# An encoder layer on one core: two of every three feed-forward tiles 4 to 15 by seven block products, with half of their weight sums made by accumulating transfers

## What is computed

```python
def swiglu(h, w_gate, w_up, w_down):          # D_MODEL 1024, D_FF 2816
    return (jax.nn.silu(h @ w_gate) * (h @ w_up)) @ w_down
h = layer_norm(DN_ALPHA * h + 0.5 * swiglu(h, ffn1_w_gate, ffn1_w_up, ffn1_w_down), g1, b1)
h = layer_norm(DN_ALPHA * h + token_mixer(h, ...), gm, bm)
h = layer_norm(DN_ALPHA * h + 0.5 * swiglu(h, ffn2_w_gate, ffn2_w_up, ffn2_w_down), g2, b2)
```

## Time and profile before

| | |
|---|---|
| median of 3 runs | 1043.09 us (1040.11 to 1043.65) |
| the profiled execution, its own time | 1039.09 us |
| its span, first to last instruction | 1037.3 us |
| granted TensorE clock, mean | 0.988 |
| busy PE / DVE / ACT / POOL | 970.1 / 760.3 / 494.8 / 52.1 us |
| bytes moved by transfers | 89.26 MB, mean 86 GB/s |

### The profile page before, as it was taken

One profiled execution on the slowest core, in us unless ns is written; L12 is line 12 of the kernel. 1 busy time (PEld: TensorE's weight loads), 2 busy tenths in 40 slices (PEclk: granted clock), 3 DMA queues, 4 the chain that ended last, 5 costly groups with the idle time before them and its releaser, 6 DMA issues.

```text
span 1037.3 us, 17455 instructions
## 1 busy us (share of the span) xinstructions
PE 970.1 (94%) x7131; PEld 693.6 (67%) x7131; DVE 760.3 (73%) x1344; ACT 494.8 (48%) x707; POOL 52.1 (5%) x96
## 2 busy tenths in 40 slices
PE   2999999999999999999997899899899999999995
PEld 1888888888788886875565437665566644434584
DVE  6877766577987676877567978878777667889634
ACT  5576655244422245763335752567666434342214
POOL 0000000000020000000000010001000000011000
PEclk9999999999999999999998989999999999999999
DMA  5233322233334300212111012122332322424002
GB/s 210 84 111 122 114 91 94 77 109 120 112 119 152 123 2 1 82 42 71 52 41 42 1 35 88 49 74 82 123 122 88 117 82 82 163 99 170 15 1 82
DMA packets 24993, 89.26 MB, mean 86 GB/s; under 512 B 3035, under 2 KB 5427, under 8 KB 24915
## 3 DMA queue, kind: packets, MB, share of 16 engines
q1 hardware_dynamic: 23904, 87.17, 24.6%
q10 hardware_dynamic: 1011, 0.99, 0.3%
HBM read 86.05 MB, written 2.10 MB: 85 GB/s over the span
## 4 chain that ended last, share of the span: by engine, by line
PE 57%; DVE 25%; ACT 10%; issue 5%; DMA 2%; POOL 1%; SPq 0%; ACTq 0%; DVEq 0%
PE PS L732 9%; PE PS L682 9%; PE PS L758 8%; PE PS L853 7%; PE PS L652 6%; DVE cmax L1793 5%; PE PS L760 4%; DVE wsp L1815 4%; PE PS L763 3%; ACT wsp L1295 2%; PE PS L827 1%; DVE big L2020 1%; ACT H L1289 1%; PE PS L1133 1%; PE PS L976 1%
## 5 line engine op out<-in xcount | busy, mean ns | idle before, releaser
L652 PE MATMUL PS<-xs,wsp 128*128 128x264 f16 (+1 forms) x1344 | 195.4, 307 | 5.6 <-DVE wsp L1815 4.5
L652 PEld LDWEIGHTS PS<-xs,wsp 128*128 128x128 f16 x1344 | 131.0, 98 | 68.9 <-DVE wsp L1815 7.9
L732 PE MATMUL PS<-xs,wsp 128*128 128x264 f16 (+1 forms) x864 | 130.9, 310 | 0.0
L1793 DVE TENSOR_REDUCE cmax<-stage 128x1 f32<-128x2048 f32 (+2 forms) x47 | 120.2, 2557 | 4.5 <-DMA stage<-in_w_out 3.6
L1295 ACT ACTIVATE wsp<-stage,wscale 128x2048 f16<-128x2048 f32 (+2 forms) x34 | 70.8, 2081 | 100.0 <-DVE wscale L1779 78.1
L732 PEld LDWEIGHTS PS<-xs,wsp 128*128 128x128 f16 x864 | 84.5, 98 | 39.9
L2681 POOL PARTITION_ALL_REDUCE call<-cmax x73 | 48.8, 669 | 894.8 <-DVE cmax L1793 652.4
L1815 DVE SCALAR_TENSOR_TENSOR wsp<-stage,wscale,wsp 128x2048 f16<-128x2048 f32 (+2 forms) x34 | 83.3, 2449 | 12.8 <-ACT wsp L1295 12.8
L758 PE MATMUL PS<-big,arena 128*128 128x264 f16 (+1 forms) x792 | 89.4, 274 | 0.0
L758 PEld LDWEIGHTS PS<-big,arena 128*128 128x128 f16 x792 | 77.5, 98 | 11.5
L763 PE MATMUL PS<-big,wsp 128*128 128x264 f16 x660 | 75.1, 276 | 1.4 <-DVE big L2020 1.3
(11 more groups left out here) (267 smaller groups left out, 1421.8 us busy)
## 6 DMA issues: line engine op xcount, KB each, us to landing
stage<-in_gate SPq DMA_DIRECT2D x44, 512.0 KB, 3.7
stage<-in_up SPq DMA_DIRECT2D x44, 512.0 KB, 4.5
stage<-in_down SPq DMA_DIRECT2D x32, 704.0 KB, 5.3
stage<-in_w_in SPq DMA_DIRECT2D x16, 512.0 KB, 4.6
stage<-in_w_out SPq DMA_DIRECT2D x8, 512.0 KB, 4.2
X<-in_x SPq DMA_DIRECT2D x4, 512.0 KB, 6.2
out_T<-H SPq DMA_DIRECT2D x16, 128.0 KB, 1.7
stage<-in_w_in SPq DMA_DIRECT2D x2, 576.0 KB, 4.8
```

The source lines that it names most:

```text
L652: return nc.tensor.matmul(dst, w, x, start=k == 0 and wp + xp == 0, stop=k == KD - 1 and xp == 1)
L732: mm = nc.tensor.matmul(dst, w, x, start=k == 0 and wp + xp == 0, stop=k == KD - 1 and xp == 1)
L1793: nc.vector.tensor_reduce(cmax[:, one], stage[:, slot, 0:cols], AX.X, ALU.max, apply_absolute_value=True).then_inc(w_max, 1)
```

## The change

Tiles 4 to 15 (`MIXED`) are worked in groups of three: tiles 4, 5, 7, 8, 10, 11, 13 and 14 by seven products, tiles 6, 9, 12 and 15 plain. That is 8 seven-product tiles in a feed-forward in place of 6. The tiles no longer go in pairs: each tile's products run one behind the other.

* **Buffers.** The chunks of tiles 4 to 15 rotate over three buffers: the two of `stage` and a third in the arena (`raw_third`). Tile 4's chunk is loaded into the third, ahead of tile 3's chunk in SP's program; in the first feed-forward behind a wait on `tok_sq`, in the second behind a wait for `x_ready` to reach its last count, which is when the last low part of the normed tokens is written.
* **Sums.** Two of the four weight sums come from transfers that POOL issues with `accum_op=ALU.add`: B11 is added onto the up block in the raw buffer (giving T1), and B22 onto a second copy of the up block, that SP loads for this (256 KB more for each seven-product tile), giving T3. Each moves 128 x 512 float32, 256 KB, inside SBUF. T2 and T4 stay on DVE as two instructions of 512 columns. Some of the sums have the other sign than before; the token sums and one scale (`up_scale`, `xinv_neg`) are negated for it.
* **Splits.** A seven-product tile has one high and one low part instruction of 2048 columns (`raw_split_hi`, `raw_split_lo`) and one of each of 1536 columns (`sums_split_hi`, `sums_split_lo`). PE's product 0 waits for the first pair alone (`raw_ready`).
* **Bounds.** `weight_sum` on ACT serves tiles 3 to 17; `chunk_max` on DVE falls away for tiles 16 and 17.

```diff
+MIXED = range(4, 16)
-SEVEN_AT = [4, 6, 8, 10, 12, 14]
+SEVEN_AT = [4, 5, 7, 8, 10, 11, 13, 14]
-SUMMED_FROM = 3
+SUMMED = range(3, 18)
+N_BUF = 3
...
+            def load_mixed(f, m):
+                i = m - MIXED[0]
+                if i == 0:
+                    if f == 0:
+                        sp.wait_ge(tok_sq, N_TOK)
+                    else:
+                        sp.wait_ge(x_ready, ln_tile(2, 2 * KD))
+                elif i < N_BUF:
+                    sp.wait_ge(w_ready, GU[f] + i + 2)
+                else:
+                    free_home(f, m - N_BUF)
+                done = mixed_loaded[buf(m)]
+                sp.dma_start(home(f, m)[:, 0:KD * P], gate[f][m]).then_inc(done, 16)
+                sp.dma_start(home(f, m)[:, KD * P:GU_COLS], up[f][m]).then_inc(done, 16)
+                if m not in SEVEN_AT:
+                    return
+                if N_BUF <= i < 2 * N_BUF:
+                    sp.wait_ge(s_ready2, 4 * f + 4)
+                elif i >= 2 * N_BUF:
+                    sp.wait_ge(w_ready, GU[f] + m - N_BUF + 1)
+                sp.dma_start(sums_at(m)[:, 0:4 * P], up[f][m][:, 0:4 * P]).then_inc(done, 16)
...
+                for m in range(2, 4):
+                    if m == 3:
+                        load_mixed(f, MIXED[0])
+                    sp.wait_ge(w_ready, GU[f] + m - 1)
+                    load_gu(f, m, (GU[f] + m) % 2)
+                for m in MIXED[1:]:
+                    load_mixed(f, m)
...
                 for m in MIXED:        # ACT, ffn(f)
+                    if m + 1 in SEVEN_AT:
+                        raw_split_hi(f, m + 1)
+                    else:
+                        gu_split_hi(f, m + 1)
+                    if m in SEVEN_AT:
+                        p1_copy(f, m)
+                    if m - 1 in SEVEN_AT:
+                        seven_gate(f, m - 1, 1)
+                    elif m > MIXED[0]:
+                        silu_tile(GU[f] + m - 1, (GU[f] + m - 1) % 2, m - 1, (m - 1) % 2, f)
+                    if m + 1 in SEVEN_AT:
+                        sums_split_hi(f, m + 1)
+                    if m + 3 in SUMMED:
+                        weight_sum(f, m + 3)
+                    hidden_sum(f, m - 1)
+                    if m in SEVEN_AT:
+                        seven_gate(f, m, 0)
...
+                for m in MIXED:        # DVE, ffn(f)
+                    if m - 1 in SEVEN_AT:
+                        product_sum(f, m - 1, 3)
+                    if m + 1 in SEVEN_AT:
+                        block_sums(f, m + 1)
+                        raw_split_lo(f, m + 1)
                     else:
+                        gu_split_lo(f, m + 1)
+                    if m - 1 in SEVEN_AT:
+                        seven_hidden(f, m - 1)
+                    elif m > MIXED[0]:
+                        hidden_tile(m - 1, (GU[f] + m - 1) % 2, (m - 1) % 2, f)
+                    out_scale_only(m + 1)
+                    if m in SEVEN_AT:
+                        product_sum(f, m, 0)
+                        product_sum(f, m, 1)
+                        product_sum(f, m, 2)
+                    if m + 1 in SEVEN_AT:
+                        sums_split_lo(f, m + 1)
+                    scale_only(m + 2)
...
+            def block_sums(f, m):      # POOL, right behind over_all(c)
+                raw = blocks(home(f, m))
+                pool.wait_ge(mixed_loaded[buf(m)], mixed_loads(f, m))
+                pool.wait_ge(w_sum, sums_through(GU[f] + m))
+                pool.dma_start(raw[:, T1, :], raw[:, B11, :], accum_op=ALU.add).then_inc(t_first[seven(f, m) % 2], 16)
+                pool.dma_start(blocks(sums_at(m))[:, T3 - N_RAW, :], raw[:, B22, :], accum_op=ALU.add).then_inc(t_first[seven(f, m) % 2], 16)
```

321 lines of the change are left out of this document (147 added, 174 removed).

## The result

The changed kernel took 1054.08 us in the median of 4 runs (1051.18 to 1057.21); the kernel before, 1042.86 beside it. The ratio is 1.0113, 95% interval 1.0077 to 1.0148: slower by 11 us, where 1041.3 was forecast with a range up to 1050.5. The same kernel once more, later: 1054.11, ratio 1.0107 (1.0057 to 1.0158).

A forecast was written before the change was run, and what follows sets the result against it. PE's matmuls, busy 94%, plus start-ups where DVE and ACT lag, were taken as the bound. First block -2.5 and second +0.7 gave -1.8 us from the 1043.1 us median: 1041.3 us, range 1037.5 to 1050.5.

The forecast's parts named there:

- PE's own work: Both feed-forwards: two more seven-product tiles in each save PE matmul time, -2.7 and -2.4, in all -5.1 us.
- The pause ahead of tile 16: PE's waits for DVE's low part ahead of tile 16 vanish: -0.3 us first block, -0.5 us second.
- Tiles 6 to 15 at no cost: Between the start-ups the reordering costs nothing; transfers go out over a tile ahead, hidden up to about 8 us.
- L: Time from the end of POOL's reduction until both accumulating transfers of a tile have landed; taken as 4.2 us.
- The start-up's waits: PE's waits up to tile 6, through DVE and ACT chains: 1.6 us first block; 1.5, 1.6, 2.5, 1.9 second.
- the transfers are slow: Rival, both start-ups: longer accumulating transfers delay tiles 4 and 5; at 6.5 us each pair, +7.4, 1050.5 us; chance 0.28.
- its formula: Slow-transfer rival, both start-ups: each microsecond of L beyond 4.2 adds about 2 us a block, 4 in all, to -1.8.
- Tile 3's load, 4.9 us late: Second block: tile 3's load, issued behind tile 4's, lands at 697.7, so ACT's weight_sum(3) starts 4.9 us late.
- my second rival: Second block: tile 3's late load does not hold it, removing +2.4: 1038.9 us, at best 1037.2; chance of faster 0.25.
- POOL's issue held by DVE: Part of the slow-transfer rival: DVE instructions delay POOL's issuing of transfers, growing L by up to 2.35 us each time.
- The range: Whole kernel: forecast time between 1037.5 us, the second rival's middle, and 1050.5 us, at L = 6.5.
- the upper bound taken for L: Two accumulating transfers wholly one behind the other, at the 4.5 us of a 512 KB load each: 9 us.

## Why the prediction was wrong

* **PE's own work, -5.1.** Right: 7179 matmuls, a tile's twelve still at 1.35 and 1.31 us wherever the clock was whole.
* **The pause ahead of tile 16, -0.3 and -0.5.** Right: both are gone.
* **Tiles 6 to 15 at no cost.** Right: no wait in either block.
* **L = 4.2 us.** This step failed. The size taken is near what an undisturbed pair shows (4.7 to 4.8, with tile 6's load held back), but I read L as a property of the transfer. It was 8.3 and 8.5 for tile 4 and 6.1 and 6.3 for tile 5, since each pair goes out beside a load of 1 MB. My own chain had both times: tile 6's load waits for tile 3's low part, which ends at 54.45 + 2.35 = 56.8, and the reduction that the pair waits for ended at 56.9. I had costed SP's loads and POOL's transfers each as if alone. The estimates of 2.6 and 3.2 us from the Trainium skill (DMA: Bandwidth & Descriptors, the anatomy of a SWDGE transfer) lie 1.5 us and more below even the undisturbed pair: the measurement decides. The page does not say that its rule holds for a transfer that adds.
* **The start-up's waits.** Predicted 1.6 us in the first block and some 7.5 in the second (1.5 ahead of tile 3, 1.6 ahead of tile 4's first product, 2.5, 1.9), measured 5.2 and 11.8. In the second block all four places and releasers were as named, with a fifth, 2.14 us for the copy ahead of index 4, that wasn't; in the first I had named only the one at index 5 (1.62 us, as predicted), and 1.23 and 2.21 us stand ahead of tile 4's first two products. (One slip of the working is too small to matter: by its own terms tile 5's reduction ends at 70.9 + 0.5 = 71.4 and not 71.9, which moves the 1.6 us by 0.3 at most.) The 7.9 us of difference are the longer L and the next point. The rival "the transfers are slow" had the right mechanism and the right side. With a mean L of 7.3 its formula gives -1.8 + 4 x 3.1 = +10.6 against +11.2 measured, but that is a coincidence of two errors: the 12.4 us by which the four L together were too long came through as some 7 us of waits, since tile 5's pair is partly covered, and the rest came from the clock.
* **Tile 3's load, 4.9 us late.** It was 6.2 us. The issue came where predicted, 5.8 us ahead of tile 2; the 2.36 MB then took 9.4 us from the first issue to ACT's start in place of 8.1, at 330 GB/s over 698 to 708 us and not the 410 of the earlier trace rows. Undoing this step alone gave 6.5 us, much more than the 2.4 that my second rival had as its worth; in the rows the second start-up lost 10.0 us by it, of which 2.5 are slow matmuls.
* **The granted clock.** No step had it, and in the profiled execution it is 5.9 us of the 13.0. In the trace of before PE's longest pause in the start-ups was 2.70 us, and the clock stood at 1.00 through both. I let PE's matmuls keep their pitch behind waits of any length.
* **POOL's issue held by DVE.** This half of the rival did not happen: the sixteen first issues of a pair took 877 to 1021 ns, and the one at 716.56, inside a DVE instruction with two SBUF inputs (716.40 to 717.62), took 890. The Trainium skill has it so (SBUF — State Buffer, Who interferes with whom): such an instruction doesn't block descriptor writing. POOL's reduction did take long, 2.35 us from 714.34 on, beside DVE's low part of tile 3 (714.14 to 716.48), where the shortest takes 0.35.
* **The range.** It ended at L = 6.5, although the upper bound taken for L was 9; by the rival's own formula 9 gives +17. The bound of the unknown was worked out and then not used.

What stays open: when the clock falls. It fell behind waits of 0.49 and 2.21 us in one trace and not behind 2.76, 3.61, 2.21 and 2.06 in another, and the same kernel had it fall at different pieces in two executions. Open too is why a load costs tile 4's pair 3.6 us and tile 5's less. The two differ in the offset between load and pair (0.1 us and 1.2 us ahead of it) and in their buffers. One trace has another offset: with tile 3's load moved back, tile 6's load goes out 1.9 us behind tile 4's pair in the second block (709.77 against 707.88), and L is 7.0 us. No run varied the offset alone.

## What to carry to other kernels

Work moved to a transfer leaves an engine's busy time and enters its waiting time: before moving it, list which instruction waits on it, what is queued behind that one in program order, and which other transfers are issued in the same microseconds. Where the pipeline was full here such transfers cost nothing, and where it started up they stood in the chain, so make the first tiles the old way, or put independent work ahead of the wait. Look behind each wait of TensorE for matmuls at the lower clock, for they can cost as much as the wait; from the wait's length alone these traces could not tell whether they would come.
